# Who adds the down-projection's bias to x1, and when the last gates are turned, in a layer with 32 experts

## The reference

```python
x = x + mixed @ w_out[layer]
h2 = rms_norm(x, moe_norm_w[layer])
# moe_ffn
logits = hf @ router_w + router_b
top_v, top_i = lax.top_k(logits, TOP_K)          # 4 of 32 experts
gates = jax.nn.softmax(top_v, axis=-1)
# tokens are sorted by expert into blocks; each block:
gu = xb @ w_gu[e] + b_gu[e]                      # 1024 -> 2048
act = (up + 1.0) * (gate * jax.nn.sigmoid(SWIGLU_ALPHA * gate))
y = act @ w_down[e] + b_down[e]                  # 1024 -> 1024
out[token] += gate_of_token * y
```

## Time and profile before

| | |
|---|---|
| median of the runs | 2202.23 us |
| profiled execution | 2205.46 us, span 2203.8 us |
| busy share of the span | TensorE 96%, VectorE 72%, ScalarE 58%, GpSimd 41% |
| head of the chain of waits | TensorE 76%, VectorE 3% |
| granted clock of TensorE, mean | 0.972 |

### The profile page before, as it was taken

The page is one execution under the profiler, slowest core; times in us unless marked ns, Lnnn a source line. Parts: engine busy times, 40 slices in busy tenths (PEclk is TensorE's granted clock), DMA queues, the critical chain, the costliest instruction groups (busy, mean ns, idle before and its releaser), DMA issues.

```text
span 2203.8 us, 39032 instructions
## 1 busy us (share of the span) xinstructions
PE 2109.1 (96%) x11205; PEld 1818.7 (83%) x11206; DVE 1596.1 (72%) x2119; ACT 1272.9 (58%) x1631; POOL 908.9 (41%) x909
## 2 busy tenths in 40 slices
PE   6999989999995999999999999999999999999995
PEld 5877767765885998988999899899887899889995
DVE  4454662553435778899888987878998987898885
ACT  4254443445334566677666766666776766776764
POOL 2014763243564334354433533333545443543532
PEclk9999999799996999999999999999999999999998
DMA  4334435302244789899877987987999987998976
GB/s 138 107 90 110 129 105 187 111 1 98 83 147 151 245 263 346 276 371 391 285 263 252 361 303 263 344 273 258 368 384 380 383 282 261 367 386 287 351 256 202
DMA packets 290265, 543.27 MB, mean 247 GB/s; under 512 B 39400, under 2 KB 51653, under 8 KB 290212
## 3 DMA queue, kind: packets, MB, share of 16 engines
q1 hardware_dynamic: 267972, 486.17, 65.3%
q0 software_dynamic: 22240, 56.42, 6.8%
HBM read 509.34 MB, written 44.14 MB: 251 GB/s over the span
## 4 chain that ended last, share of the span: by engine, by line
PE 76%; DVE 3%; issue 1%; DMA 1%; ACT 1%; SPq 0%; POOL 0%; DVEq 0%; ACTq 0%; POOLq 0%
PE banks L2613 17%; PE banks L208 12%; PE banks L210 11%; PE banks L209 11%; PE banks L2615 7%; PE banks L1996 3%; PE banks L2549 2%; PE banks L2548 2%; PE banks L1284 1%; PE banks L2612 1%; DVE VL L1263 1%; PE banks L1982 1%; PE banks L1981 1%; PE banks L2104 1%; PE banks L2553 1%
## 5 line engine op out<-in xcount | busy, mean ns | idle before, releaser
L1263 DVE TENSOR_TENSOR VL<-RAW,VH 128x2048 fp32r<-128x2048 f32 x389 | 881.8, 2286 | 29.8 <-ACT VH L1258 24.3
L1258 ACT ACTIVATE VH<-RAW 128x2048 fp32r<-128x2048 f32 x390 | 733.2, 1910 | 108.2 <-PE banks L210 81.7
L2613 PE MATMUL banks<-T,VH 128*128 128x384 f32 x1920 | 542.0, 357 | 1.8 <-DVE T L1304 1.8
L2615 PE MATMUL banks<-T,VL 128*128 128x192 f32 x1680 | 422.1, 251 | 0.0
L2613 PEld LDWEIGHTS banks<-T,VH 128*128 128x128 f32 x1920 | 345.7, 189 | 2.7 <-issue 2.2
L2615 PEld LDWEIGHTS banks<-T,VL 128*128 128x128 f32 x1680 | 321.6, 191 | 0.5
L2308 POOL DMA_INDIRECT out<-yb,ycur x32 | 74.7, 2335 | 417.9 <-DVE yb L2452 400.7
L209 PE MATMUL banks<-VL,T 128*128 128x512 f32 x544 | 211.9, 389 | 0.0
L208 PE MATMUL banks<-VH,T 128*128 128x512 f32 x544 | 211.9, 389 | 0.0
L210 PE MATMUL banks<-VH,T 128*128 128x512 f32 x544 | 211.8, 389 | 0.0
L208 PE MATMUL banks<-VH,A 128*128 128x512 f32 x512 | 204.7, 400 | 4.2 <-DVE A L2432 3.1
(11 more groups left out here) (389 smaller groups left out, 4073.2 us busy)
## 6 DMA issues: line engine op xcount, KB each, us to landing
RAW<-in_expert_w_gate_up SPq DMA_DIRECT2D x528, 512.0 KB
RAW<-in_expert_w_down SPq DMA_DIRECT2D x262, 512.0 KB
RW<-in_w_in SPq DMA_DIRECT2D x24, 512.0 KB, 5.5
xin<-in_x SPq DMA_DIRECT2D x8, 512.0 KB, 10.1
MBC<-dM SPq DMA_DIRECT2D x8, 512.0 KB, 10.9
dQ<-parts SPq DMA_DIRECT2D x8, 512.0 KB, 3.0
dK<-parts SPq DMA_DIRECT2D x8, 512.0 KB, 3.0
WRAW<-in_w_out SPq DMA_DIRECT2D x8, 512.0 KB, 8.2
```

The source lines that it names most:

```text
L1258: act.activation(VH[:, i, ks], RAW[:, i, ks], ACT.Copy).then_inc(s_hi, 1)
L1263: dve.tensor_tensor(VL[:, i, ks], RAW[:, i, ks], VH[:, i, ks].bitcast(f32), ALU.subtract).then_inc(s_w, 1)
L2613: last = pe.matmul(o[:, 0:2 * NW], VH[:, c % 3, k, col], T2[:, k], start=k == 0, stop=k == KT - 1)
L2615: pe.matmul(o[:, HI_ALL], VL[:, c % 3, k, col], T2[:, k, HI_ALL], start=False, stop=False)
```

## The change

1. TensorE runs the router of tile 7 without waiting for the gates of tile 6. The turns of the gates of tiles 6 and 7 and their bias products stand behind the rank products.
2. VectorE adds the bias product to x1 straight from PSUM, in two halves of 512 columns. ScalarE's copies to yd and GpSimd's adds are gone, and so is yd.
3. In the loop VectorE's adds for tile t - 3 stand at the head of turn t, behind the inverse of the gates' sum. The adds of tile 5 stand between h2 of tile 7 and the routing of tile 7; those of tiles 6 and 7 stand between the one-hots and the table. The first half of chunk 0's remainder ('split_lo(dve, 0, 0, 1)') has moved there too, ahead of the table.
4. ScalarE copies btT before it keeps the gates of tile 6.
5. e4 has two buffers, and the one-hot tiles lie 40 KB higher, since VL's first part is now written earlier.

```diff
@@ layout
-    yd = r4e.take("yd", [P, D])
+    r4e.take("spare", [P, D])
-    r5w = Region(A_X + 64 * KB, 10 * KB)
+    r5w = Region(A_X + 104 * KB, 10 * KB)
@@ SyncE
             def finished(u):
-                sp.wait_ge(s_xo, u + 1)
+                sp.wait_ge(s_yd, 2 * u + 2)
                 sp.dma_start(out2[tok(u), :], x1[:, u % XB]).then_inc(s_st[u % 2], 16)
@@ GpSimd
-            def biased(u):
-                pool.wait_ge(s_yd, 2 * u + 2)
-                pool.wait_ge(s_rT, 2 * u + 2)
-                if u == TT - 1:
-                    pool.wait_ge(s_h2, TT)
-                pool.tensor_tensor(x1[:, u % XB], x1[:, u % XB], yd[:], ALU.add).then_inc(s_xo, 1)
...
             gates(TT - 1)
-            biased(TT - 2)
-            biased(TT - 1)
@@ ScalarE
-            def bias_out(u, c, bank):
-                act.wait_ge(s_gb, 2 * u + c + 1)
-                if c == 0 and u >= 1:
-                    act.wait_ge(s_xo, u)
-                act.activation(yd[:, c * CH:(c + 1) * CH], bank, ACT.Copy).then_inc(s_yd, 1)
...
             exponents(TT - 2)
-            gates_kept(TT - 2)
...
             exponents(TT - 1)
+            act.wait_ge(s_ex, TT)
             for q in range(2):
                 act.activation(btT[:, :, 4 * q:4 * q + 4], ps[q][:, 0:8 * NE].rearrange("p (g i e) -> p g i e", g=2, i=4), ACT.Copy).then_inc(s_btT, 1)
-            for c in range(2):
-                bias_out(TT - 2, c, ps[2 + c])
+            gates_kept(TT - 2)
             gates_kept(TT - 1)
             split_first(1, 1)
-            for c in range(2):
-                bias_out(TT - 1, c, ps[c])
@@ VectorE
+            def biased(u, c, bank):
+                dve.wait_ge(s_gb, 2 * u + c + 1)
+                if c == 0:
+                    dve.wait_ge(s_ss, u + 1)
+                    dve.wait_ge(s_h2, u + 1)
+                    dve.wait_ge(s_rT, 2 * u + 2)
+                x = x1[:, u % XB, c * CH:(c + 1) * CH]
+                dve.tensor_tensor(x, x, bank, ALU.add).then_inc(s_yd, 1)
...
                 if t >= 2:
                     inverse(t - 2)
+                if t >= 3:
+                    biased(t - 3, 0, ps[5])
+                    biased(t - 3, 1, ps[5])
                 residual(t, 0)
...
+            for c in range(2):
+                biased(TT - 3, c, ps[c])
+            route(last)
             inverse(TT - 2)
-            route(last)
             inverse(TT - 1)
...
+            for c in range(2):
+                biased(TT - 2, c, ps[2 + c])
+            for c in range(2):
+                biased(TT - 1, c, ps[c])
+            split_lo(dve, 0, 0, 1)
             link(dve.tensor_scalar(ns[:, 0:1], ns[:, 0:1], 1.0, None, ALU.max))
...
-            split_lo(dve, 0, 0, 1)
             split_lo(dve, 0, 1, 2)
@@ TensorE
             def router(t):
-                if t >= 1:
+                if 1 <= t < TT - 1:
                     pe.wait_ge(s_gt, t)
...
             turn(TT - 1, 1)
-            pe.wait_ge(s_h2T, 2 * (TT - 1) + 1)
-            gates_turned(TT - 2)
             router(TT - 1)
...
             last.then_inc(s_bT, 1)
-            for c in range(2):
-                down_bias(TT - 2, c, ps[2 + c])
...
             pe.matmul(ps[6][:, (TT - 1) * NE:TT * NE], beforeR[:], selS[:, TT - 1], start=False, stop=True).then_inc(s_rank, 1)
+            gates_turned(TT - 2)
+            for c in range(2):
+                down_bias(TT - 2, c, ps[2 + c])
             gates_turned(TT - 1)
```

More of the change, by code:

```diff
@@ L1151, in layer_kernel @@
     m8 = r5.take("m8", [P, TT, 8])
-    e4 = r5.take("e4", [P, TOPK])
+    e4 = r5.take("e4", [P, 2, TOPK])
     negm = r5.take("negm", [P, TT])
@@ L1329, in stage3 @@
         s_tab, s_tb, s_ix, s_ixz = s5("tabs"), s5("tab_rows"), s5("idx"), s5("idx_zero")
-        s_ex, s_zr, s_G, s_gT, s_gt, s_gb, s_yd, s_xo = (s5(n) for n in ("exponents", "inverse_sums", "gates", "gates_turned", "gates_kept", "down_bias", "bias_out", "x1_biased"))
+        s_ex, s_zr, s_G, s_gT, s_gt, s_gb, s_yd = (s5(n) for n in ("exponents", "inverse_sums", "gates", "gates_turned", "gates_kept", "down_bias", "bias_out"))
         s_bd, s_bhi, s_blo = s5("down_rows"), s5("down_hi"), s5("down_lo")
@@ L1499, in on_gpsimd @@
                     gates(t - 1)
-                    biased(t - 2)
                     continue
@@ L1507, in on_gpsimd @@
                     gates(t - 1)
-                if t >= 2:
-                    biased(t - 2)
             gates(TT - 1)
-            biased(TT - 2)
-            biased(TT - 1)
             for i in range(2):
@@ L1613, in exponents @@
                 act.wait_ge(s_sel, u + 1)
-                act.activation(e4[:], m8[:, u, 0:TOPK], ACT.Exp, bias=negm[:, u:u + 1], accum_out=zsum[:, u:u + 1])
+                act.activation(e4[:, u % 2], m8[:, u, 0:TOPK], ACT.Exp, bias=negm[:, u:u + 1], accum_out=zsum[:, u:u + 1])
                 act.activation(G[:, u], logits[:, u], ACT.Exp, bias=negm[:, u:u + 1]).then_inc(s_ex, 1)
@@ L1619, in gates_kept @@
                 act.activation(GT[0:3 * NE], ps[4][0:3 * NE, P:2 * P], ACT.Copy).then_inc(s_gt, 1)
-            def bias_out(u, c, bank):
-                act.wait_ge(s_gb, 2 * u + c + 1)
-                if c == 0 and u >= 1:
-                    act.wait_ge(s_xo, u)
-                act.activation(yd[:, c * CH:(c + 1) * CH], bank, ACT.Copy).then_inc(s_yd, 1)
             for t in range(TT):
-                if t >= 3:
-                    bias_out(t - 3, 0, ps[5])
                 if t >= 2:
                     exponents(t - 2)
-                if t >= 3:
-                    bias_out(t - 3, 1, ps[5])
                 if t + 1 < TT:
@@ L1654, in on_scalar @@
             turned_out(TT - 1, 1)
-            for c in range(2):
-                bias_out(TT - 3, c, ps[c])
             exponents(TT - 2)
-            gates_kept(TT - 2)
             def split_first(c, hf):
```

## The result

The changed kernel took 2190.11 us, median of 6 runs (2186.43 to 2196.63); the kernel before, run beside it, 2203.28 (2201.95 to 2207.07). The ratio is 0.9938, with a 95% interval of 0.9920 to 0.9956: 13 us faster, between 9.7 and 17.6. Predicted were 2190.4 and a gain of 11.8. Measured once more, in another job, the changed kernel took 2192.93 (median of 6) beside 2205.3, 12.4 us less. The profiled execution took 2190.53 us (span 2188.8), against 2205.46 (2203.8) before.

The account below looks back on a forecast made before the run. Only TensorE's gaps before the first expert product were taken to pay: 6.0 + 3.9 + 2.1 - 0.2 = 11.8 us off the median 2202.23 gave 2190.4. The parts' bounds, 2187.5 to 2193.5, were opened to 2187.0 to 2196.5.

Parts of the forecast that it names:

- Part 1: Tile 7's router no longer waits for tile 6's gates; block counts come 6.0 us earlier (bounds 5.8 and 6.3).
- Between the two engines' answers: Time taken for the block counts: 678.0, between VectorE ready at 677.7 and TensorE's release at 678.2.
- Part 2: Without GpSimd's bias adds, two stalls in VectorE's count chain go; 3.9 us gained (2.8 to 4.3).
- The charge of 0.4 for the gates: Cost taken for GpSimd's gates of tiles 6 and 7 meeting VectorE's count chain: 0.4 us, up to 1.5.
- TensorE in front of the list: TensorE may be late for VectorE's first one-hot by 1.0 us at the lower clock; charged 0, 1.0 a bound.
- Part 3: From the last one-hot to the first expert product, 2.1 us gained (0 to 2.6).
- The legs: Two paths from the opening scan's old place to the first expert product: table about 14.7, gather 14.5 to 15.3; 15.0 taken.
- At nothing: Loop adds, x1 stores, chunk 3's load and earlier stores and loads expected to be covered; only 0.2 us charged (0 to 1.0).
- Gather 2 stays slow: Rival: GpSimd's second gather keeps its 5.04 us, the last stretch gains nothing; 9.7 us gained, 2192.5; chance 0.12.
- Late for the list: Rival: TensorE or GpSimd starts the list loop 3 to 4 us late; 8 us gained, 2194.2; chance 0.11.
- The port against the change: Rival: GpSimd's multiplies hold VectorE's PSUM adds, VectorE's chain holds GpSimd's gates; 5.6 us slower, 2207.8; chance 0.03.

Follow-up runs that it names:

- e1: Changed kernel with tile 7's router again waiting for tile 6's gates, their turn, copy and bias pair in the old place; 2198.98 us, ratio 0.9963.
- e2: Changed kernel with two idle GpSimd adds of a scratch tile to itself behind the last gates, and one fill in turn 5; 2193.78 us, ratio 0.9952.
- e5: Kernel before with only the first half of chunk 0's remainder moved ahead of the table, one-hot tiles in their higher place; 2197.89 us, ratio 0.9972.
- e4: Changed kernel with the first half of chunk 0's remainder put back behind the table; 2191.39 us, ratio 0.9939.
- e6: Changed kernel with the first half of chunk 0's remainder earlier still, ahead of the routing of tile 7; 2191.12 us, ratio 0.9941.
- e8: Changed kernel without VectorE's four bias adds for tiles 6 and 7, their bias product missing from the output; 2195.88 us, one run.
- e3: Changed kernel with four GpSimd memsets of a scratch tile behind the last gates, and one fill in turn 5; 2188.79 us, one run.
- e9: Changed kernel with both halves of chunk 0's remainder behind the table and 70 unused warm-up products on TensorE; 2196.9 us, ratio 0.9958.

## Why the prediction was right

**Part 1** was forecast at 6.0 us and is 5.71 (also by e1), just below its bounds. The router was over at 672.27, earlier than the 673.4 to 675.2 that I gave: its first half, which reads only the first h2T copy, ran from 669.72, and the second at full clock. I had let the whole router start behind the second copy. For the clock, the windows of the changed kernel (columns as in the earlier trace rows) give 1.00 from 672 to 673, 0.66 in the next and 0.50 in the third (it fell once TensorE stood).

```profile
672.00:673.00 1.00, 0.27 (x3) 0.15 (x2) 1.00 (x2) 1.00 (x1) 0.00 (x0) 1.00 0.00 0
673.00:674.00 1.00, 0.00 (x0) 0.00 (x0) 1.00 (x2) 0.42 (x1) 0.00 (x0) 0.66 0.23 94
674.00:675.00 1.00, 0.71 (x14) 0.74 (x15) 0.90 (x7) 0.00 (x0) 0.00 (x0) 0.50 1.02 422
```

What is late next was named rightly: VectorE's second add releases the bias transposes 2.63 us behind h2 (2.7 forecast). From there TensorE needed 3.57 us to the counts at the low clock, not 3.4, and VectorE, ready after 5.27, waited 0.92. "Between the two engines' answers" was the wrong choice: the later one sets it.

**Part 2** was forecast at 3.9 and is 4.22. The stalls were GpSimd's adds, 4.3 us, as e2 shows by bringing adds back. The charge of 0.4 for the gates was too high: with the gates of tile 6 out of the way (e1) the chain takes 6.09 us, with both 6.18, so 0.1.

**TensorE in front of the list** was charged 0. It was ready 0.51 us ahead of VectorE's first one-hot.

**Part 3** was forecast at 2.1 and is 2.74. The gathers went as worked out: the first 3.07 us, held until the subtraction ended, the second 1.04. The legs were 0.6 too long: 15.0 was counted from the scan's old place, 0.8 behind the last one-hot, which makes 15.8, and 15.15 were measured. All twelve transposes took 2.79 us in one row, where I had added 1.94 and a later leg of up to 4.1. What ends the stretch is the transposes at 0.50, ScalarE's T and VectorE's T; the transposes themselves started 0.17 us behind the table's last product, when the first gather had landed, so that the two legs ended together. What I had wrong is why: I gave the gain to the subtraction's move. e5 shows that the move alone is worth 3.73 us, e4 that with the adds in place it is worth -0.63, because it now makes gather 1 and the table late.

**At nothing.** The loop's adds were charged 0.2 us and cost 0.08: from the first residual add of the loop to the last are 108.15 us before (558.58 to 666.73) and 108.23 after (558.06 to 666.29). In turn 6 the adds stand at 641.88 and 643.25, 0.69 us each, the second beside GpSimd's multiply (642.83 to 645.22), and the weight load that waits for the first comes at 642.62; it had come at 643.05 in the trace before, which ran 0.45 us later there. The stores of x1 landed in 3.8 us (median; 2.9 before), and ScalarE's copies of chunk 2 began behind them at 696.99 and took 3.71 us, ahead of the first tokens' copy at 702.90. The load of chunk 3 left 2.9 us before the product; ScalarE took it 11.6 behind the product, and nothing waited.

**The rivals.** "Gather 2 stays slow" fell by e5, where the stretch would have stayed at 17.89 us. "Late for the list" did not come (0.51 us to spare). "The port against the change" fell with the adds' 0.68 to 0.69 us, all sixteen alike: the add with one input in PSUM that met a GpSimd multiply was not held, and GpSimd's ten operations ran from 676.28 to 679.18. Gained are 12.7 us by stretches and 13.2 by medians, where 11.8 were forecast.

**Where luck helped.** The three parts were off by -0.3, +0.3 and +0.6 us. That the median is within 0.3 us of the forecast is more than the method gives: the same kernel took 2192.93 in the other job. The range was summed wrongly, too. The bounds of the parts add up to gains of 13.2 and 7.6 us, so 2189.0 to 2194.6, or 2195.6 with the 1.0 us kept for the list, and not 2187.5 (which adds something for a high clock without a price) to 2193.5; the result would have been inside either.

## What to carry to other kernels

Where a short VectorE instruction takes ten times its usual time, look for the GpSimd instruction that ends with it, and give the large element-wise work to VectorE with one input in PSUM. It works the other way too: VectorE's large two-input subtractions hold GpSimd's gathers and its smallest instructions, so place them where GpSimd issues nothing that the end waits for. Judge such a move after the others: one edit had already freed what the next was to free.

## What the runs showed that I had not expected

- A subtraction on VectorE with both inputs in SBUF holds an indirect DMA on GpSimd: 5.04 us before and 3.07 after, against 1.32 and 1.04 free in e4, e5, e6 and e8. The Trainium skill, "SBUF — State Buffer", section "Who interferes with whom", infers that tensor_tensor does not stop descriptor generation. Here a tensor_tensor held the gather, and the measurement decides. Whether it was the writing of the descriptors that waited, or the reading of the gather's indices in SBUF, no run here shows. A later gather is held longer still: 6.75 us (from 707.98 in e4), beneath three subtractions that end at 713.82.
- Writes of GpSimd alone held a TENSOR_SCALAR of 128x32 (1.07 us for 0.18) and left two-input forms alone (e3).
- Full clock behind the first product brought TensorE to the end of the first block 1.6 us earlier (56.22 and 56.23 us for 57.82), but it then stood 2.3 to 2.4 us before the second. With e9, which arrived no earlier and stood 3.4, the three kernels with warm-ups stop there and no other does, for a reason that these runs leave open.
